# Input norm's chains ahead of the evictions of unscaled tiles, and attention scores as two fp32r products with query and rest stacked over 128 rows

## The reference

```
h = concat(meta, x)                                   # 528 x 1024
z = rmsnorm(h, norm1);  proj = z @ w_in               # q, f, i, og, pool, gates
h += (sigmoid(ga) * (hgrn2(q, f, i, og) @ w_a) + sigmoid(gb) * (pool(p) @ w_b)) @ w_out
h += gated_conv_ffn(rmsnorm(h, norm2));  x = rmsnorm(h, final)[16:]
for layer in (0, 1):                                  # 512 tokens, 12 heads of 64
    z = rmsnorm(x, norm_mix)
    q, k, v, qm = split(z @ w_in)
    # layer 0: window of +-128 tokens, 4 key heads, ALiBi, sink; layer 1: 8 x 16 grid window, 12 key heads, bias
    p = softmax(q @ k^T / 8 + bias);  y_tok = p @ v
    y_mem = softmax(qm @ mk^T / 8) @ mv               # 4 heads, 256 memory tokens
    x += concat(y_tok, y_mem) @ w_out
    x += (silu(g) * u) @ w_down,  g, u = split(rmsnorm(x, norm_ffn) @ w_gate_up)
return rmsnorm(x, norm_final)
```

## Time and profile before

| | us |
|---|---|
| median of 3 runs | 2104.51 (2104.12 to 2259.88) |
| profiled execution, whole | 2103.05 |
| its span, first to last instruction | 2101.2 |
| PE busy | 2068.2 (98%), 11899 matmuls |
| DVE, ACT, POOL busy | 1066.3, 845.7, 189.4 (51%, 40%, 9%) |
| start to the first projection's matmuls | 19.37 |
| attention stages, PE's first score to last value product | 967.4 to 1054, 1585 to 1672 |

### The profile page before, as it was taken

One profiled execution on the slowest core, in us unless ns is written; L12 is line 12 of the kernel. 1 busy time (PEld: TensorE's weight loads), 2 busy tenths in 40 slices (PEclk: granted clock), 3 DMA queues, 4 the chain that ended last, 5 costly groups with the idle time before them and its releaser, 6 DMA issues.

```text
span 2101.2 us, 32292 instructions
## 1 busy us (share of the span) xinstructions
PE 2068.2 (98%) x11899; PEld 1798.9 (86%) x11899; DVE 1066.3 (51%) x1788; ACT 845.7 (40%) x1323; POOL 189.4 (9%) x176
## 2 busy tenths in 40 slices
PE   7999999999999999999999999999999999999998
PEld 7999999999988888888888888888888888888887
DVE  4224777555652666546654433444435654433443
ACT  5534444543222544445733222334435643322333
POOL 0003000110110000101000000110104001100100
PEclk9999999999999999999999999999999999999999
DMA  4322111123333333331023332333322033333332
GB/s 129 104 85 80 41 41 41 55 87 92 96 98 109 90 90 107 94 110 51 1 61 99 91 105 85 99 105 96 90 81 73 3 90 90 102 99 87 93 99 81
DMA packets 321919, 174.98 MB, mean 83 GB/s; under 512 B 6560, under 2 KB 319136, under 8 KB 321840
## 3 DMA queue, kind: packets, MB, share of 16 engines
q1 hardware_dynamic: 321840, 173.92, 28.4%
HBM read 171.80 MB, written 2.10 MB: 83 GB/s over the span
## 4 chain that ended last, share of the span: by engine, by line
PE 68%; DVE 1%; issue 1%; ACT 0%; POOL 0%; POOLq 0%; DVEq 0%; ACTq 0%
PE ps L1901 38%; PE ps L1907 19%; PE ps L2396 3%; PE ps L2420 3%; PE ps L2376 2%; PE ps L2405 2%; PE ps L2346 0%; PE ps L2454 0%; PE ps L2017 0%; ACT w_hi L711 0%; PE ps L2259 0%; DVE w_lo L1192 0%; PE ps L2007 0%; PE ps L2312 0%; PE ps L2333 0%
## 5 line engine op out<-in xcount | busy, mean ns | idle before, releaser
L1192 DVE TENSOR_TENSOR w_lo<-raw,w_hi 128x1024 fp32r<-128x1024 f32 (+2 forms) x298 | 383.9, 1289 | 520.1 <-ACT w_hi L711 518.8
L1901 PE MATMUL ps<-z_hi,w_hi 128*128 128x512 f32 (+2 forms) x2128 | 643.5, 343 | 4.1 <-ACT w_hi L711 2.6
L1901 PE MATMUL ps<-z_lo,w_hi 128*128 128x512 f32 (+2 forms) x2128 | 634.5, 338 | 0.0
L711 ACT ACTIVATE w_hi<-raw 128x1024 fp32r<-128x1024 f32 (+2 forms) x298 | 328.4, 1102 | 465.5 <-PE ps L1907 417.1
L1907 PE MATMUL ps<-z_hi,w_lo 128*128 128x512 f32 (+2 forms) x2128 | 443.8, 339 | 0.0
L1901 PEld LDWEIGHTS ps<-z_hi,w_hi 128*128 128x128 f32 x2128 | 366.3, 188 | 56.0 <-issue 4.5
L1901 PEld LDWEIGHTS ps<-z_lo,w_hi 128*128 128x128 f32 x2128 | 365.1, 188 | 44.8
L1907 PEld LDWEIGHTS ps<-z_hi,w_lo 128*128 128x128 f32 x2128 | 344.2, 188 | 45.2
L1901 PE MATMUL ps<-g_hi,w_hi 128*128 128x512 f32 (+1 forms) x539 | 209.4, 390 | 0.5 <-POOL g_lo L643 0.5
L1901 PE MATMUL ps<-g_lo,w_hi 128*128 128x512 f32 (+1 forms) x539 | 208.8, 389 | 0.0
L643 POOL TENSOR_TENSOR g_lo<-gv,g_hi 128x512 f32 x66 | 85.7, 1298 | 1082.6 <-ACT g_hi L1048 1082.6
(11 more groups left out here) (311 smaller groups left out, 2334.2 us busy)
## 6 DMA issues: line engine op xcount, KB each, us to landing
raw<-w_gate_up SPq DMA_DIRECT2D x88, 512.0 KB, 3.7
raw<-w_down SPq DMA_DIRECT2D x48, 704.0 KB, 4.3
raw<-w_in SPq DMA_DIRECT2D x44, 512.0 KB, 3.7
raw<-w_up SPq DMA_DIRECT2D x44, 512.0 KB, 3.7
raw<-w_out SPq DMA_DIRECT2D x24, 512.0 KB, 3.7
raw<-w_in_b SPq DMA_DIRECT2D x14, 512.0 KB, 3.6
raw<-w_in_a SPq DMA_DIRECT2D x12, 512.0 KB, 3.6
raw<-w_branch SPq DMA_DIRECT2D x8, 512.0 KB, 3.7
```

Of the source, the lines that this page charges most:

```text
L711: act.activation(w_hi[s][:, 0:width], raw[s][:, 0:width], ACT.Copy).then_inc(hi_done, 1)
L1192: dve.tensor_tensor(w_lo[s][:, 0:width], raw[s][:, 0:width], w_hi[s][:, 0:width].bitcast(F32), ALU.subtract).then_inc(lo_done, 1)
L1901: pe.matmul(out, w_hi[s][:, w0 + k * P:w0 + (k + 1) * P], rhs[:, lo:lo + width], start=a, stop=False)
```

## The change

At the start the first `row_inverse` stands ahead of all tile copies and its root on ACT directly behind the squares that it needs; only chunk 0 is turned there. Chunks 1 and 2 are turned behind unit 0, chunk 3 inside unit 1, and the three tiles are copied behind the splits of unit 1. Chunks 2 and 3 of the scaled rows are made in halves, by ACT and POOL and by two DVE operations. The Exp and the lower bounds that follow it move to the value stage. In attention, ACT copies into scratch tiles (`scaled_heads`), DVE scales there, ACT rounds (`rounded_heads`) and DVE subtracts (`rest_heads`); queries hold the rounded part in rows 0 to 63 and the rest in rows 64 to 127, keys the rounded part in both halves of `k_hi` and the rest in both of `k_lo`, so that two fp32r products over 128 rows give the score. Memory heads stay fp32. Buffers move for it: y lies over the queries, and two of the three `rpb_raw` in the last part of `w_hi`, so layer 1's 24 bias DMAs come after its first two weight loads and wait for the last down unit.

```diff
+        w_at = [fixed[0] + 4 * SLOT * i for i in range(2)]
...
-        q_heads = sb(at, "q_heads", [P, QH + MH, SEQ])
-        k_heads = sb(at, "k_heads", [P, QH, SEQ])
+        q_pair = sb(at, "q_pair", [P, QH, SEQ], F32R)
+        q_mem = sb(at, "q_mem", [P, MH, SEQ])
+        y_heads = sb([region], "y_heads", [P, AH, SEQ])
+        k_hi = sb(at, "k_hi", [P, QH, SEQ], F32R)
+        k_lo = sb(at, "k_lo", [P, QH, SEQ], F32R)
         v_tok = sb(at, "v_tok", [P, 4, QH * HD])
-        y_tok = sb(at, "y_tok", [P, 4, D])
-        at[0] = max(at[0], memory_end)
-        bias = [sb(at, "bias0", [P, GRID_R * (48 + 32 + 32)])]
-        rpb_raw = [sb(at, f"rpb_raw{i}", [P, GRID_R, 48]) for i in range(2)] + [rpb_last]
...
+        bias = [sb([scratch], "bias0", [P, GRID_R * (48 + 32 + 32)])]
+        rpb_raw = [sb([w_at[i] + 4 * UNIT], f"rpb_raw{i}", [P, GRID_R, 48]) for i in range(2)] + [rpb_last]
...
+        def x_bank(c):
+            return ps[(0, 2, 3, 2)[c]]
...
+        def y_slot(head):
+            return chunked(y_heads[:, head // 2 * 2, :], 4)[:, :, head % 2 * HD:(head % 2 + 1) * HD]
...
-                if l == 1:
-                    for r in range(3):
-                        bias_load(r, r)
                 w = (t["w_in_a_2"], t["w_in_b_2"])[l][0]
                 qkw = (QH + (KVA, QH)[l]) * HD
                 vw = (KVA, QH)[l] * HD
                 n = UNITS[f"qk{l}"]
-                with sp.Fori(0, qkw // (2 * P)) as i:
-                    load(n + 2 * i, 0, cols(w, i * (2 * P)))
-                    load(n + 2 * i + 1, 1, cols(w, i * (2 * P) + P))
+                load(n, 0, cols(w, 0))
+                load(n + 1, 1, cols(w, P))
+                if l == 1:
+                    sp.wait_ge(used, n + 2)
+                    for r in range(3):
+                        bias_load(r, r)
+                with sp.Fori(0, qkw // (2 * P) - 1) as i:
+                    load(n + 2 * i + 2, 0, cols(w, i * (2 * P) + 2 * P))
+                    load(n + 2 * i + 3, 1, cols(w, i * (2 * P) + 3 * P))
...
-            for c in range(2):
-                if c == 0:
-                    pool.wait_ge(n1["inv"], 6)
-                pool.tensor_scalar(z_rows[:, c, :], x_rows[:, c, :], first_scale(c + 1), 1.0, ALU.mult, ALU.mult)\
+            for c in range(3):
+                lo = 0 if c < 2 else D // 2
+                if c != 1:
+                    pool.wait_ge(n1["inv"], (6, 0, 12)[c])
+                pool.tensor_scalar(z_rows[:, c, lo:], x_rows[:, c, lo:], first_scale(c + 1), 1.0, ALU.mult, ALU.mult)\
                     .then_inc(n1["rows_pool"], 1)
...
-                pool.memset(q_heads[HD:, :, :], 0.0).then_inc(s["zero"], 1)
+                pool.memset(q_mem[HD:, :, :], 0.0).then_inc(s["zero"], 1)
                 pool.wait_ge(*s.at("zero", 1))
                 pool.wait_ge(att_loaded, 16)
+                pool.wait_ge(*s.at("q_lo", (8, 12)[l]))
...
             row_squares(1)
+            row_root(0, 3, 0)
             row_squares(2)
-            row_root(0, 3, 0)
             row_squares(3)
             row_root(3, 2, 6)
             split_hi(0, 0)
             act.wait_ge(n1["inv"], 12)
-            act.activation(z_rows[:, 2, :], x_rows[:, 2, :], ACT.Identity, scale=first_scale(3))\
+            act.activation(z_rows[:, 2, 0:D // 2], x_rows[:, 2, 0:D // 2], ACT.Identity, scale=first_scale(3))\
                .then_inc(n1["rows_act"], 1)
...
+            act.preload_act_table_set("natural_log_exp_and_others")
+            act.wait_ge(lb_step, 3)
+            act.activation(lbc[:, 2:4, :], lbc[:, 0:2, :], ACT.Exp).then_inc(lb_step, 1)
...
+                queries, keys, s = 6, (2, 6)[l], atts[l]
+                def rounded_heads(m):
+                    act.wait_ge(*s.at("scaled", m + 1))
+                    if m < queries:
+                        hi, tile = q_pair[0:HD, 2 * m:2 * m + 2, :], scaled_heads[m % 2][0:HD, :, :]
+                    else:
+                        hi, tile = k_hi[:, 2 * (m - queries):2 * (m - queries) + 2, :], scaled_heads[m % 2][:, :, :]
+                    act.activation(hi, tile, ACT.Copy).then_inc(s["q_hi"], 1)
+                for m in range(queries + keys + 2):
+                    half = m % 2
+                    if 1 <= m <= queries + keys:
+                        rounded_heads(m - 1)
+                    if m == 0 and l == 1:
+                        late_root(norm_a[l], SEQ)
+                    split_hi(n + m + 2, half, WIDTHS[n + m + 2])
+                    if m == 0 and l == 1:
+                        late_scale(norm_a[l], SEQ, att_scale)
+                    act.wait_ge(used, n + m + 3)
+                    if 2 <= m < queries + keys:
+                        act.wait_ge(*s.at("q_lo", m - 1))
+                    for j in range(2):
+                        heads = ps[half][j * HD:(j + 1) * HD, 0:1, :]
+                        if m < queries:
+                            x = act.activation(scaled_heads[half][0:HD, j:j + 1, :], heads, ACT.Copy, scale=HD ** -0.5)
+                        elif m < queries + keys:
+                            for rows in (slice(0, HD), slice(HD, P)):
+                                x = act.activation(scaled_heads[half][rows, j:j + 1, :], heads, ACT.Copy)
                         else:
+                            head = 2 * (m - queries - keys) + j
+                            x = act.activation(q_mem[0:HD, head:head + 1, :], heads, ACT.Copy, scale=HD ** -0.5)
+                    x.then_inc(ps_free[half], 1)
...
+            row_inverse(0, 3, 0, 3)
             copied(0)
-            copied(1)
-            row_inverse(0, 3, 0, 3)
-            copied(2)
...
+            for lo in (0, D // 2):
+                dve.tensor_scalar(z_rows[:, 3, lo:lo + D // 2], x_rows[:, 3, lo:lo + D // 2], first_scale(4), 1.0,
+                                  ALU.mult, ALU.mult).then_inc(n1["rows_dve"], 1)
...
-            copied(3)
+            for c in range(1, CHUNKS):
+                copied(c)
...
-                        tiles = q_heads[0:HD, 2 * m:2 * m + 2, :]
+                        tiles, rows = scaled_heads[s_][0:HD, :, :], HD
                     elif m < first_key + keys:
-                        tiles = k_heads[:, 2 * (m - first_key):2 * (m - first_key) + 2, :]
+                        tiles, rows = scaled_heads[s_][:, :, :], P
                     else:
-                        head = QH + 2 * (m - first_key - keys)
-                        tiles = q_heads[0:HD, head:head + 2, :]
-                    rows = P if first_key <= m < first_key + keys else HD
-                    dve.tensor_tensor(tiles, tiles, row_scale[0:rows, 0:SEQ].rearrange("p (o n) -> p o n", o=1)
+                        head = 2 * (m - first_key - keys)
+                        tiles, rows = q_mem[0:HD, head:head + 2, :], HD
+                    dve.tensor_tensor(tiles, tiles, att_scale[0:rows, 0:SEQ].rearrange("p (o n) -> p o n", o=1)
                                       .to_broadcast([rows, 2, SEQ]), ALU.mult).then_inc(s["scaled"], 1)
+                def rest_heads(m):
+                    dve.wait_ge(*s.at("q_hi", m + 1))
+                    if m < first_key:
+                        tile, hi = scaled_heads[m % 2][0:HD, :, :], q_pair[0:HD, 2 * m:2 * m + 2, :]
+                        lo = q_pair[HD:, 2 * m:2 * m + 2, :]
+                    else:
+                        tile, hi = scaled_heads[m % 2][:, :, :], k_hi[:, 2 * (m - first_key):2 * (m - first_key) + 2, :]
+                        lo = k_lo[:, 2 * (m - first_key):2 * (m - first_key) + 2, :]
+                    dve.tensor_tensor(lo, tile, hi.bitcast(F32), ALU.subtract).then_inc(s["q_lo"], 1)
                 pairs = (5, 7)[l]
                 if l:
                     late_mean(norm_a[l], SEQ)
                     late_inverse(norm_a[l], SEQ)
-                for i in range(pairs):
-                    width = UNIT if i < pairs - 1 else WIDTHS[UNITS[f"v{l}"]]
-                    split_lo(n + 2 * i + 2, 0, width)
-                    if i == 0:
+                for m in range(2 * pairs):
+                    if 1 <= m <= first_key + keys:
+                        rest_heads(m - 1)
+                    split_lo(n + m + 2, m % 2, WIDTHS[n + m + 2])
+                    if m == 0:
                         dve.wait_ge(*norm_a[l].at("copied", 1))
-                    if i > 0:
-                        scaled(2 * i - 1)
-                    split_lo(n + 2 * i + 3, 1, width)
-                    scaled(2 * i)
-                last_scaled = 2 * pairs - 1
+                    scaled(m)
...
-            for c in range(3):
-                pe.wait_ge(x_loaded[c], 16)
-                x_turn(c)
+            pe.wait_ge(x_loaded[0], 16)
+            x_turn(0)
             pe.wait_ge(n1["inv"], 6)
             pe.wait_ge(x_copied, 1)
             pe.matmul(ps[0][:, 0, 0:META], first_scale(0, META).to_broadcast([META, P]), ident[0:META, 0:META],
                       start=True, stop=True).then_inc(n1["meta_wide"], 1)
```

(35 more changed lines are left out.)

75 lines of the change are left out of this document (23 added, 52 removed).

## The result

The changed kernel takes 2089.82 us (median of 4 runs, 2088.28 to 2091.14), the one before 2104.32: a ratio of 0.9936, 95% interval 0.9924 to 0.9948. That is 0.64% less, inside the 2% of "no change"; the median is 1.2 us above the 2088.6 that were forecast. One of the four runs of the kernel before was in a slower state (2259.88 us) and isn't in the ratio. The profiled execution took 2088.28 us, its span is 2086.5 against 2101.2: 14.7 us less, where the steps had summed to 15.9.

The account below looks back on a forecast made before the run. PE's stream of matmuls was taken to bound the kernel. Start -1.9, attention -20.8, projections +0.5 and layer 1's hole +6.3 summed to -15.9 us, giving 2088.6 us on the median's scale, range 2081 to 2099.

Parts of the forecast that it names:

- The hole in layer 1: Layer 1's third projection unit: its weight load queues behind 24 bias DMAs; 4.7 us hole plus low clock, 6.3 us together.
- 1.6 us: Behind layer 1's projection hole: one low-clock stretch of 3.3 us granted 0.5, half of it lost.
- the bound for a second stretch: Layer 1's projection hole: upper bound of 8.5 us if the low clock level lasts a second stretch.
- Rival (a): Layer 1's projection: the bias DMAs don't hold the weight load up, so no hole; 2082.3 us, chance 0.12.
- The attention: Attention scores: two fp32r products replace each fp32 one, step 5.29 to 4.30 us; 10.4 us less per layer, 20.8 for both.
- half a us per layer: Attention's first heads: deducted from the gain because the first 1.8 us of the first full step fall at the low clock.
- Rival (b): Head loop: the round trip PE, ACT, PE or DVE sets the step, 4.7 us; 2096.6 us, chance 0.14.
- (c): Head loops: attention loses the full clock as transposes become 1.1 of 4.3 us a step; up to 2175 us, chance 0.03.
- (d): Attention scores: the score products win nothing because their weights are exposed; 2109 us, chance 0.03.
- The start: First projection: the hole ahead of unit 2 shrinks, PE resuming at about 33.8 us instead of 35.70; 1.9 us less.
- The projections: Query and key projections: added ACT and DVE work, a key unit 5.9 us round on ACT; 0.5 us more in all.
- the us that the range held for it: The start: 1 us allowed in the range in case fewer early transposes make the clock rise later.

Follow-up runs that it names:

- the lots: Changed kernel with layer 1's 24 bias DMAs in three lots of 8 behind the 4th, 6th and 8th weight load: 2080.50 us, ratio 0.9886.
- the filled kernel: Changed kernel with ten extra, unread fp32r products of 512 columns per attention stage ahead of PE's first wait for row_max: 2086.57 us, ratio 0.9921.

## Why the prediction was right

The forecast of 2088.6 us was 1.2 short, and the shape is the forecast one: 20 us won in the attention, a third of it lost again in a hole that the move of the bias DMAs opened. Step by step:

**The hole in layer 1, +6.3 in the sum, +7.2 measured.** The mechanism was right link by link: SP's order, an issue at 1468.70 (the forecast's 1481.3 lies 11.5 behind the last down unit, which ended at 1457.3 here: 1468.8), a landing after 3.77, split, three copies. For the forecast delay of 4.7 us the trace has 4.6 against before, and 5.2 against the stage without a hole. What was mis-sized is the term "1.6 us" for the clock behind it: I took one stretch of 3.3 us as after the attention's hole, and it was 6.8 us long, 5.34 of them with PE at work at 0.50, which is 2.6 us. 5.2 and 2.6 are the 7.8 us that the lots gave back. The range held this case (by its own terms the bound for a second stretch is 4.7 + 1.6 + 1.6 = 7.9, not 8.5). Rival (a), no hole, is out, and the lots show what it would have been: 2080.5.

**The attention, -20.8 in the sum, -20.0 measured.** The step was right to 0.02 us, and so were the products' prices. The expected 0.05 us of contention a step in layer 0 isn't there. Half of the difference is these 0.02 us, twenty times. The other half lies in the first heads, "half a us per layer" for the clock: layer 1's longer low stretch cost 0.8 us, as the filled kernel shows, and layer 0's nothing. Rival (b), a step set by the round trip, has its place and its reason as stated, DVE's slow negation in layer 0, but only from 4.20 us down; the forecast had 0.12 us of air there, less than I thought. Rivals (c) and (d) are out: the head loop runs at 1.00 behind its entry, with transposes as 1.1 of its 4.32 us, and the products have the price of their columns. The Trainium skill says that the full clock doesn't engage for transposes (TensorE: Matmul & The Clock Gate, Part 4: PE-mode transpose). A loop that is three quarters products doesn't test that; the start does, and differs: there the level rose while PE had only transposes.

**The start, -1.9 in the sum, -2.3 measured, and here several sizes were wrong.** The first chain ends at 9.25 us, not 9.86, as the input landed 0.6 earlier in that execution; that says nothing of the change. PE resumed unit 2 at 33.12 on the mean of eleven profiles, not 33.8: "at 1.53 / 12 us each" was too dear for the transposes, since a row's duration reaches past the start of the next one; 16 of them add 25.17 - 23.51 = 1.66 us, not 2.05, and 8 in unit 1 0.79. The tile copy inside unit 1 therefore came at 29.27 instead of 30.1, and everything behind it on DVE. That the Exp holds the split and makes the next copy load a table was right. So was that the chains' order wins next to nothing: the prediction books "2.2 us" for it and hands them back on PE, and the run with the old order has PE at the value products within 0.75 us. In the new order the Exp would cost more than in the old, 5.3 us against a hole of 2.64, because it waits for the last copy; only in this sense are the two edits one. "Without that cover it would cost its table load, over a us" was far too low: three table loads and a low clock.

**The projections, +0.5 in the sum.** Not there. A key unit on ACT takes 1517.26 - 1511.52 = 5.74 us round, not 5.9, and no unit after the third comes late:

```profile
1511.52 1.04 ACT L731 ACTIVATE w_hi<-raw 128x1024 fp32r<-128x1024 f32 x1
...
1517.26 1.05 ACT L731 ACTIVATE w_hi<-raw 128x1024 fp32r<-128x1024 f32 x1
```

The remaining 0.3 us stand behind the attention of layer 1 (428.8 us to the end, before 428.4); the profiles differ there by as much, 428.4 to 429.0.

## What to carry to other kernels

In an in-order DMA queue, ask of a block of transfers not how long it is but when the first load behind it is wanted: the same 11 us cost 7.8 us behind the 2nd load and nothing behind the 3rd. A function that needs another ACT table belongs where ACT is idle, and its price is that of all loads around it plus what waits behind. And before taking more work off the bounding engine, look for the floor of the round trip beside it: here one layer's floor was 0.12 us away, the other's 0.6 or more.

## What I had not expected of the hardware

- The same place shows low stretches of different length in different executions: the entry of layer 0's attention has 3.4 us in the changed kernel and 6.8 in the one with three lots, whose code there is the same, and the stage takes 77.1 or 78.8 us with it.
- What a low stretch costs depends on who is late: at that entry 3.4 us of it cost nothing (77.13 with, 77.17 without), for PE waits for the softmax anyway; behind the hole in layer 1, with PE at work throughout, it cost half its length.
- Idle time ahead of it isn't the whole condition. In the memory stage PE waits 2.15 us at one place in all fourteen profiles; a low stretch of 3.4 us stands there in eight of them and none in six. And in the old order of the start (two profiles) the level falls from 1.00 to 0.50 at 13.4 and 13.7 us, with PE turning rows between waits of 0.8 to 1.5 us. Why was not tried.
- The windows say 1.00 for the first 14 us of the new start, but the pace says otherwise: until some point between 14 and 17.3 us transposes follow each other every 0.213 us, behind it and for the rest of the start every 0.11, as these two rows show (24 and 16 of them). The rise comes before or within the first projection matmuls, so the us that the range held for it wasn't needed.

```profile
11.03 5.62 PE L1995 MATMUL ps<-con,z_rows 128*128 128x128 f32 x24
...
23.51 1.91 PE L1989 MATMUL ps<-con,x_rows 128*128 128x128 f32 x16
```

- A DVE instruction on 128x4 elements takes 0.89 us when a bias product of POOL runs beside it and 0.22 when none does (nine and three steps of layer 0, in three kernels), and through it POOL sets layer 0's step in the kernel with one score product.
